# Dilated attention: the copy of the output from PSUM moves from ScalarE to VectorE, and the copy to the stage moves in front of VectorE's reads, one step later

## The reference

```python
DIL_HEADS = 8
DIL_PATTERNS = ((128, 1), (512, 4), (2048, 16))
...
    s = jnp.einsum('bnqche,bnkche->bnchqk', qs, kw).astype(jnp.float32) * scale + bias
    s = jnp.where(mask, s, MASK_VALUE)
    m = jnp.max(s, axis=-1, keepdims=True)
    e = jnp.exp(s - m)
    l = jnp.sum(e, axis=-1, keepdims=True)
    o = jnp.einsum('bnchqk,bnkche->bnqche', e.astype(v.dtype), vw)
    inv_l = (1.0 / l[..., 0]).transpose(0, 1, 4, 2, 3)[..., None]
    o = (o.astype(jnp.float32) * inv_l).reshape(B, Lp, H, Dh)[:, :S]
...
def dilated_attention(q, k, v, slopes):
    """Mixture of dilation patterns merged by their softmax denominators."""
...
    w = jax.nn.softmax(jnp.stack(lses, axis=0), axis=0)
    out = jnp.sum(w[..., None] * jnp.stack(outs, axis=0), axis=0)
```

## Time and profile before

| | |
|---|---|
| median of 3 runs | 2876.13 us (2876.09 to 2876.19) |
| the profiled execution's own time | 2868.93 us |
| its span, first to last instruction | 2867.1 us |
| mean granted TensorE clock | 0.974 |
| TensorE busy (matmuls) | 2688.6 us, 94% |
| VectorE busy | 2032.5 us, 71% |
| ScalarE busy | 1593.3 us, 56% |
| GpSimd busy | 1049.9 us, 37% |

### The profile page before, as it was taken

How to read it: one execution, slowest core, us unless ns; L and a number is a source line. 1 busy time by engine, 2 the same in 40 slices (tenths; PEclk the granted TensorE clock), 3 DMA queues, 4 the chain that set the end, 5 groups by cost and what they waited for, 6 DMA issues and landing times. The chain is left out here.

```text
span 2867.1 us, 54253 instructions
## 1 busy us (share of the span) xinstructions
PE 2688.6 (94%) x20642; PEld 2219.0 (77%) x20642; DVE 2032.5 (71%) x3611; ACT 1593.3 (56%) x3210; POOL 1049.9 (37%) x790
## 2 busy tenths in 40 slices
PE   7899989999799999989997998999899999899998
PEld 5678867888599999977775777788677788677776
DVE  5767687666799999978887775433667767567775
ACT  6575446644588888879997122322433433555553
POOL 4667656777322212119761443200011011312111
PEclk9999999999899999999998999999999999899999
DMA  3432323333411120014445667142265466634441
GB/s 118 130 109 87 101 82 96 111 105 103 118 40 40 41 62 25 25 39 143 128 128 175 207 216 258 66 137 76 66 176 130 99 173 177 185 124 147 149 149 67
DMA packets 317295, 330.11 MB, mean 115 GB/s; under 512 B 24384, under 2 KB 259952, under 8 KB 313840
## 3 DMA queue, kind: packets, MB, share of 16 engines
q1 hardware_dynamic: 287184, 292.85, 33.6%
q0 software_dynamic: 6912, 23.07, 2.8%
q10 hardware_dynamic: 22944, 10.76, 1.7%
HBM read 217.13 MB, written 109.47 MB: 114 GB/s over the span
## 5 line engine op out<-in xcount | busy, mean ns | idle before, releaser
L1061 PE MATMUL p_acc<-p_y_hi,p_x_hi 128*128 128x512 f32 x904 | 362.6, 401 | 11.8 <-DVE p_y_lo L843 3.8
L1061 PE MATMUL p_acc<-p_y_lo,p_x_hi 128*128 128x512 f32 x904 | 356.3, 394 | 0.0
L1061 PE MATMUL p_acc<-p_y_hi,p_x_lo 128*128 128x512 f32 x904 | 356.1, 394 | 0.0
L563 POOL TENSOR_TENSOR p_x_lo<-k_carry,p_x_hi 128x1024 fp32r<-128x1024 f32 x113 | 279.6, 2481 | 132.1 <-ACT p_x_hi L635 132.1
L2106 PEld LDWEIGHTS d_out<-d_v,d_w_t 64*128 64x128 f32 x4096 | 260.2, 187 | 17.4 <-ACT d_a_parts L1941 13.1
L2106 PE MATMUL d_out<-d_v,d_w_t 64*128 64x128 f32 x4096 | 267.9, 274 | 1.2 <-ACT d_a_parts L1941 1.2
L1926 ACT ACTIVATE d_e<-d_e,d_neg_top 128x2048 f32<-128x2048 f32 x128 | 257.0, 2008 | 20.2 <-DVE d_neg_top L2013 20.2
L924 DVE RECIPROCAL p_aux<-p_aux 128x512 f32<-128x512 f32 x64 | 215.1, 3361 | 53.7 <-ACT p_aux L731 53.7
L1596 PE MATMUL s_acc<-h_y_hi,s_x_hi 128*128 128x512 f32 x560 | 224.7, 401 | 25.2 <-DVE s_x_lo L1400 14.7
L1596 PE MATMUL s_acc<-h_y_hi,s_x_lo 128*128 128x512 f32 x560 | 221.2, 395 | 0.0
L1596 PE MATMUL s_acc<-h_y_lo,s_x_hi 128*128 128x512 f32 x560 | 221.2, 395 | 0.0
(11 more groups left out here) (370 smaller groups left out, 7175.6 us busy)
## 6 DMA issues: line engine op xcount, KB each, us to landing
k_carry<-in_w_in SPq DMA_DIRECT2D x128, 256.0 KB, 3.3
k_carry<-in_a_w_in POOLq DMA_DIRECT2D x72, 256.0 KB, 3.6
cols<-p_z SPq DMA_DIRECT2D x64, 256.0 KB, 2.5
o_parts<-l_stage SPq DMA_DIRECT2D x192, 66.0 KB, 1.8
m_o<-o_parts SPq DMA_DIRECT2D x48, 264.0 KB, 6.1
k_carry<-cols SPq DMA_DIRECT2D x48, 256.0 KB, 4.6
j_x_second<-x SPq DMA_DIRECT2D x20, 512.0 KB, 3.7
k_carry<-x SPq DMA_DIRECT2D x20, 512.0 KB, 3.7
```

The source lines that it names most:

```text
L563: pool.tensor_tensor(x_lo[:, m % RING], inputs.place(x_place(m)), x_hi[:, m % RING].bitcast(F32), ALU.subtract).then_inc(x_lo_made, 1)
L1061: mm = pe.matmul(bank_of(n, j), x_part[:, n % RING, j, kt], y_part[:, y_slot(n), kt], start=(kt == 0 and m == 0 and not (g == 0 and n % 2 ...
```

## The change

The copy of the output (`copy_out`) leaves ScalarE's loop and becomes a `tensor_copy` in VectorE's loop, as the last thing of a pass, behind the four reads of `top(n+2)`. The stage copy goes from the end of the pass to the place right behind the move, and there it is for step n-3 instead of n-2; the loop has one pass more. TensorE's, SyncE's and GpSimd's orders stay, and all waits stay with the operations that have them.

```diff
--- before.py
+++ after.py
@@ -2379,22 +2379,13 @@
                     act.wait_ge(valued, n - 1)
                 act.activation(turned_to(n, side), turned_from(n, side), ACT.Copy).then_inc(moved_act, 1)
 
-            def copy_out(n):
-                act.wait_ge(valued, n + 1)
-                if n >= 2:
-                    act.wait_ge(o_turned, n - 1)
-                act.activation(o_t[:, n % 2].rearrange("p u n -> p (u n)"), out[:, 0, 0:2 * P], ACT.Copy).then_inc(o_copied, 1)
-
             exp(0)
             exp(1)
-            for n in range(TOTAL + 1):
+            for n in range(TOTAL):
                 if n + 1 < TOTAL:
                     exp(2 * n + 2)
                     exp(2 * n + 3)
-                if n < TOTAL:
-                    move(n, 0)
-                if n >= 1:
-                    copy_out(n - 1)
+                move(n, 0)
 
         @block.vector
         def _(dve):
@@ -2427,6 +2418,12 @@
                     dve.wait_ge(valued, n - 1)
                 dve.tensor_copy(turned_to(n, side), turned_from(n, side)).then_inc(moved_dve, 1)
 
+            def copy_out(n):
+                dve.wait_ge(valued, n + 1)
+                if n >= 2:
+                    dve.wait_ge(o_turned, n - 1)
+                dve.tensor_copy(o_t[:, n % 2].rearrange("p u n -> p (u n)"), out[:, 0, 0:2 * P]).then_inc(o_copied, 1)
+
             def stage_out(n):
                 dve.wait_ge(o_turned, n + 1)
                 dve.tensor_copy(stage[:, 2 * n % SLOTS:2 * n % SLOTS + 2, 0:2 * HD],
@@ -2435,13 +2432,15 @@
             bias.wait_made(dve)
             top(0)
             top(1)
-            for n in range(TOTAL + 2):
+            for n in range(TOTAL + 3):
                 if n < TOTAL:
                     move(n, 1)
+                if n >= 3:
+                    stage_out(n - 3)
                 if n + 2 < TOTAL:
                     top(n + 2)
-                if n >= 2:
-                    stage_out(n - 2)
+                if 1 <= n < TOTAL + 1:
+                    copy_out(n - 1)
 
         @block.tensor
         def _(pe):
```

## The result

| | before | changed |
|---|---|---|
| median of the runs | 2876.11 us (2869.34 to 2876.19, 4 runs) | 2895.09 us (2892.95 to 2900.12, 4 runs) |
| ratio, with its 95% interval | | 1.0082 (1.007 to 1.0094) |
| the profiled execution | 2868.93 us | 2894.47 us |
| its span | 2867.1 us | 2892.7 us |
| the stage, first T to the end of the last stage copy | 264.7 us | 289.0 us |

The changed kernel is slower, by 19.0 us by the medians and by 25.5 us by the two profiled executions; 24.3 of these 25.5 lie in the stage. The forecast was 2897.1, range 2889 to 2907.

A forecast was written before the change was run, and what follows sets the result against it. Bound before: a two-step loop over TensorE and ScalarE's output copy. The moved stage copy's chain makes the stage 276.3 us against 255.3, +21.0; 2868.93 becomes 2889.9, plus 7.2 carried over 2897.1 us, range 2889 to 2907.

The forecast's parts named there:

- T: TensorE's transposes of a step (line 2479); T to T in wide steps forecast at 3.26 us, against 2.92.
- What bounds the kernel before: Loop over V, ScalarE's copy, four exponentials, move and T: two wide steps take 5.84 us, 2.92 each; TensorE needs 2.80.
- V: TensorE's value matmuls of a step (line 2496); V to T forecast at 1.03 us wide, 0.59 narrow.
- O: TensorE's turn of an earlier output (line 2505); forecast to start 1.86 us after T in wide steps, before 1.41.
- VectorE's part at nothing: VectorE's 96 added copies make its wide step 2.68 us, below TensorE's 2.80, so they cost nothing.
- The chain: T, move, stage copy, O, V, next T within one step: wide 3.26 us against 2.92, narrow 2.30 against 2.26.
- The sum: Stage from the fourth T: 92 intervals make 270.6 us, with the end 276.3 against 255.3, so +21.0 us.
- The 7.2 us carried over: Whole kernel: median 2876.13 us lies 7.2 above the profiled execution; carried over, 2889.9 becomes 2897.1.
- Rival 1: VectorE instructions don't overlap across the move; stage copy starts 0.08 later in some 93 chains: +7.4, 2904.5 us; chance 0.12.
- Rivals 2 and 3: Stage copy in time, ScalarE loop gone: 2864 us, chance 0.05; O late by only 0.12, time stays 2876: chance 0.04.
- Rival 4: Granted clock falls as TensorE is busy 86% of a step: 0.4 more per T, 30 us or more; chance 0.03.
- The slots and stores: Output's store issued some 1.7 us later, counted at nothing; only longest landing could delay narrow reads, up to some 2 us.

The follow-up runs named there:

- Values first in the kernel before: Kernel before with values(n-1) in front of turn_out(n-2) on TensorE, output copy still on ScalarE: 2859.58 us, ratio 0.995; again 2861.62 us.
- the stage copy put back: Changed kernel with the stage copy behind the reads again, for step n-2, output copy staying on VectorE: 2858.98 us, ratio 0.9949 to the kernel before.
- values first: Changed kernel with values(n-1) in front of turn_out(n-2) on TensorE: 2856.46 us, ratio 0.9942 to the kernel before; second time 2860.22 us.
- the copy in front of the move: Changed kernel with the stage copy of step n-3 in front of move n on VectorE: 2861.08 us, ratio 0.9962 to the kernel before.

## Why the prediction was right

*What bounds the kernel before.* Right: a loop of two steps over V, ScalarE's copy, exponentials and move. Values first in the kernel before took O's 0.37 out of the loop, the stage copy put back took ScalarE's copy out of it, and either way it no longer ruled.

*VectorE's part at nothing.* Right, shown by three runs: with 96 more copies on VectorE, T to T is 2.80. The stage copy put back, values first and the copy in front of the move take 12 to 18 us off the kernel before.

*The chain.* Right in place and in cause, and each link can be compared:

| link, wide step | forecast | measured |
|---|---|---|
| T to move | 0.75 | 0.75 |
| move to stage copy | 0.61 | 0.61 |
| stage copy | 0.42 | 0.41 |
| its end to O | 0.08 | 0.15 |
| O to V | 0.37 | 0.34 |
| V to T | 1.03 | 1.03 |
| sum | 3.26 | 3.29 |

One link lies outside the bounds that the forecast gave it: from VectorE's end to O it is 0.15, in all 95 places between 0.14 and 0.16, and not 0.06 to 0.11. Two links that came out shorter, the stage copy by 0.01 and O to V by 0.03, took part of that back. The forecast says that no row of the stage had a step from VectorE to TensorE; the trace before has one at the stage's entry, from VectorE's split of the keys (start 1281.82, 2.28 long) to the first scores at 1284.16, 0.06. It would not have helped: it belongs to another instruction of TensorE with another wait, and the last section shows that this matters.

*The sum.* From the fourth T (1297.53) to the last stage copy's end (1577.52) it took 280.0 us; 276.3 had been forecast. Of the 3.7 missing, 0.03 in each of 65 wide intervals make 2.0 and 0.035 in each of 27 narrow ones 0.9. At the three pair changes the last narrow interval was 2.48 instead of 2.33, 0.4 in all; there, wide reads fill VectorE in a narrow step. At the end I had stage copy 93 done before output copy 94; it stands behind it in VectorE's queue, 0.4:

```profile
1571.36 0.46 PE L2478 MATMUL l_turn<-k_ident,l_e 64*128 64x64 f32 x8
...
1573.81 0.43 DVE L2425 COPY l_o_t<-l_out 128x256 f32<-128x256 f32 x1 [1.19 <-PE l_out L2495]
1574.15 0.41 DVE L2429 COPY l_stage<-l_out 128x256 f32<-128x256 f32 x1
...
1574.71 0.41 PE L2504 MATMUL l_out<-k_ident,l_o_t 128*128 128x128 f32 x2 [0.95 <-DVE l_stage L2429]
...
1577.10 0.42 DVE L2429 COPY l_stage<-l_out 128x256 f32<-128x256 f32 x1 [0.59 <-PE l_out L2504]
```

The last T is at 1571.36 and the end at 1577.52: 6.16, not 5.73. The first three steps were 0.4 shorter than before. So a stage longer by 24.3 us, where 21.0 was the forecast, and 1.2 outside it.

*The 7.2 us carried over.* This step was weak: it took the distance between a median and a single execution for something fixed, and it is by luck that the forecast comes out within 2.0 us. The before kernel's four runs lie at 2869.34 and at 2876.1, and its later ones everywhere from 2868.6 to 2876.3, while the profiled execution was at the low end. The changed kernel's median lies only 0.6 above its profiled execution, so 6.6 of the 7.2 were too much. The 4.6 that were missing (3.3 in the stage, the rest outside it) went the other way. From profiled execution to profiled execution the forecast was +21.0, and +25.5 was measured. The rest of the program is not quite constant: behind the stage it took 1313.8 us in the profile before and 1315.2 in the changed one. Whether the change has a part in these 1.4 is open; they are small against the 8 us over which the kernel before spreads by itself.

*Rival 1*, no overlap of move and stage copy, is refuted as it was put: the starts are 0.61 apart. The three links from the move on are 0.61 + 0.41 + 0.15 = 1.17. By this sum alone, VectorE's full emptying, which the Trainium skill describes ("VectorE: DVE Perf Modes", The DRAIN you can't avoid), would fit about as well, with 0.69 for the move, 0.42 for the copy and 0.06 to O, also 1.17. But the rows of the last section speak against reading the 0.15 that way. *Rivals 2 and 3* are refuted by 95 waits of O. These add up to 36.7 us where 25 to 30 were forecast; the wide steps' 0.44 alone make some 27, and the narrow steps' 0.18 and the end's 0.95, three times, bring it near the total. *Rival 4*: the granted clock of the stage stayed at 0.99, the same as in the earlier trace rows, though TensorE is busy for 87% of it.

*The slots and stores.* No wait of VectorE for a store shows up in the changed kernel's list. With values first, in shorter steps, there are two, 0.6 us in all in the first trace and 1.8 in the second.

## What to carry to other kernels

Before an instruction is moved earlier in an in-order queue, look at what the instruction in front of it waits for. "Earlier" was behind a move that waits for this pass's transposes, so a copy that had been done a pass ahead became a link of a chain through one pass. Write such a chain down link by link for one step, and compare it with the engine's own work for a step; busy shares (84% and 78% here) show nothing of it. And where an engine waits for something that is ready later in the pass, look first for independent work standing behind it in its own queue: exchanging two neighbours was worth 39 us on TensorE (values in front of the output's turn) and 34 on VectorE (the stage copy in front of the move), both against the changed kernel.

## What was not expected of the hardware

From a copy's end in the rows to the start of TensorE's instruction that waits for it, it is 0.05 or 0.06 us in some places and 0.14 to 0.16 in others. The stage copy to O is of the second kind in all 95 places of the changed kernel. A first thought is that the rows of overlapped copies flatter VectorE: the stage copy starts 0.08 before the move in front of it ends, and the extra 0.09 would give that back. The other runs' rows don't bear this out. In the run with the stage copy put back, this output copy starts 0.08 before the stage copy in front of it ends, and O follows its end (1354.41) after 0.05:

```profile
1353.66 0.42 DVE L2429 COPY l_stage<-l_out 128x256 f32<-128x256 f32 x1
1354.00 0.41 DVE L2425 COPY l_o_t<-l_out 128x256 f32<-128x256 f32 x1
...
1354.46 0.44 PE L2504 MATMUL l_out<-k_ident,l_o_t 128*128 128x128 f32 x2 [0.20 <-DVE l_o_t L2425]
```

And in the run with values first on TensorE, this stage copy starts only when the copy in front of it has ended (1537.46), and O follows its end (1537.89) after 0.15:

```profile
1537.04 0.42 DVE L2425 COPY l_o_t<-l_out 128x256 f32<-128x256 f32 x1 [0.17 <-PE l_out L2495]
1537.46 0.43 DVE L2429 COPY l_stage<-l_out 128x256 f32<-128x256 f32 x1
...
1538.04 0.41 PE L2504 MATMUL l_out<-k_ident,l_o_t 128*128 128x128 f32 x2 [0.61 <-DVE l_stage L2429]
```

Nor does it go by the engine that copies. O behind an output copy follows after 0.05 or 0.06, whether VectorE made it (six places with the stage copy put back) or ScalarE (1550.83 to 1550.89 in the earlier trace rows). V behind an output copy follows after 0.15, whether VectorE made it (1390.24 to 1390.39, in the second run of the changed kernel with values first) or ScalarE (1540.68 to 1540.83, in the kernel before with values first). So in these rows the gap goes with TensorE's instruction and with what it waits for. Why it does is open; no run was made for it. For a forecast it means: take the gap from a row in which the same instruction waits for the same semaphore, and where there is none, keep 0.05 to 0.16 as the bounds.
